# Another merge order for the retention and gated-linear mixers of a two-block network on one core

## The reference, cut to what matters

```python
def hybrid_mixer(h, hc, w_in, ret_decay, gate_up, gate_b, gla_norm_g, ...):
    lat, cx = project_in(h, w_in), project_in(hc, w_in)
    r_lat, r_ctx = bidirectional_scan(retention_inputs(lat, True), retention_inputs(cx, False))
    g_lat, g_ctx = bidirectional_scan(gla_inputs(lat), gla_inputs(cx))
    def merge(r, g, parts):
        ret = from_heads(head_layernorm(r)) * jax.nn.silu(parts[3])
        gla = from_heads(rmsnorm(g, gla_norm_g)) * jax.nn.silu(parts[7])
        return jnp.concatenate([ret, gla], axis=-1)
```

## Time and profile before

| what | us |
|---|---|
| median of three runs | 3759.76 (3759.74 to 3764.34) |
| the profiled execution, its own time | 3764.54 |
| its span in the profile | 3762.7 |
| mixer of layer 0, span time 2009.8 to 2249.9 | 240.1 |
| mixer of layer 1, span time 3127.1 to 3324.6 | 197.5 |

### The profile page before, as it was taken

How to read it: one execution, slowest core, us unless ns; L and a number is a source line. 1 busy time by engine, 2 the same in 40 slices (tenths; PEclk the granted TensorE clock), 3 DMA queues, 4 the chain that set the end, 5 groups by cost and what they waited for, 6 DMA issues and landing times.

```text
span 3762.7 us, 42305 instructions
## 1 busy us (share of the span) xinstructions
PE 3543.3 (94%) x17448; PEld 2805.7 (75%) x17448; DVE 2017.1 (54%) x3717; ACT 1232.1 (33%) x2053; POOL 212.6 (6%) x302
## 2 busy tenths in 40 slices
PE   7999899999989999998999989999998998879998
PEld 6657678887867678887986557888887885558886
DVE  5565588856654588854126664323235236654344
ACT  4353343234453333233112222332233212134332
POOL 0200000001040000000000001000001000000000
PEclk9999999999999999999999859999999998789999
DMA  4302155522202145533210011212122220112331
GB/s 164 115 12 79 45 168 179 167 91 84 74 27 78 45 157 172 168 119 124 81 57 27 26 38 46 79 57 68 57 66 86 99 68 17 40 45 90 101 91 67
DMA packets 214108, 317.01 MB, mean 84 GB/s; under 512 B 5304, under 2 KB 162618, under 8 KB 212636
## 3 DMA queue, kind: packets, MB, share of 16 engines
q1 hardware_dynamic: 198108, 243.00, 19.9%
q0 software_dynamic: 15808, 71.31, 5.6%
HBM read 300.66 MB, written 14.49 MB: 84 GB/s over the span
## 4 chain that ended last, share of the span: by engine, by line
PE 83%; DVE 11%; ACT 4%; issue 2%; DMA 1%; POOL 0%; SPq 0%; DVEq 0%; ACTq 0%; POOLq 0%
PE ps L94 82%; DVE t L115 5%; ACT t L100 3%; DVE t L107 3%; PE ps L97 1%; DVE t L111 1%; DVE ps L107 0%; DVE ps L115 0%; DVE t L121 0%; DVE t L112 0%; DMA t<-gates_away 0%; DVE t L125 0%; DVE ps L112 0%; DVE t L118 0%; DMA t<-in_mem 0%
## 5 line engine op out<-in xcount | busy, mean ns | idle before, releaser
L94 PE MATMUL ps<-t,t 128*128 128x512 f32 (+7 forms) x17032 | 3486.5, 368 | 193.5 <-DVE t L107 98.1
L94 PEld LDWEIGHTS ps<-t,t 128*128 128x128 f32 (+3 forms) x17032 | 2753.2, 191 | 900.4 <-issue 177.3
L100 ACT ACTIVATE t<-t 128x1024 fp32r<-128x1024 f32 (+6 forms) x1168 | 831.0, 744 | 1226.7 <-PE ps L94 653.5
L107 DVE TENSOR_TENSOR t<-t,t 128x1024 fp32r<-128x1024 f32 (+5 forms) x882 | 781.7, 911 | 708.9 <-ACT t L100 693.5
L100 ACT ACTIVATE t<-ps 128x512 f32<-128x512 f32 (+5 forms) x490 | 248.5, 531 | 1062.7 <-PE ps L94 1027.7
L115 DVE SCALAR_TENSOR_TENSOR t<-t,t,t 128x256 f32<-128x256 f32 (+4 forms) x935 | 438.7, 530 | 7.6 <-ACT t L100 1.2
L107 DVE TENSOR_TENSOR t<-ps,t 128x512 f32<-128x512 f32 (+4 forms) x293 | 187.4, 659 | 248.2 <-PE ps L94 181.8
L115 DVE SCALAR_TENSOR_TENSOR t<-ps,t,t 128x512 f32<-128x512 f32 (+1 forms) x228 | 139.7, 662 | 279.7 <-PE ps L94 259.6
L107 POOL TENSOR_TENSOR t<-t,t 128x64 f32<-128x64 f32 (+1 forms) x196 | 129.3, 684 | 1724.9 <-ACT t L100 1721.6
L118 DVE COPY t<-ps 128x256 f32<-128x256 f32 (+3 forms) x169 | 75.9, 477 | 276.8 <-PE ps L94 256.7
L100 ACT ACTIVATE t<-ps,t 128x512 f32<-128x512 f32 (+3 forms) x106 | 61.6, 582 | 131.9 <-PE ps L94 94.6
(11 more groups left out here) (31 smaller groups left out, 293.3 us busy)
## 6 DMA issues: line engine op xcount, KB each, us to landing
t<-in_w_ff SPq DMA_DIRECT2D x64, 1024.0 KB, 7.6
t<-in_w_mlp SPq DMA_DIRECT2D x64, 1024.0 KB, 5.4
t<-in_ada_w POOLq DMA_DIRECT2D x48, 1024.0 KB, 5.9
t<-in_w_in SPq DMA_DIRECT2D x30, 1024.0 KB, 5.3
t<-in_w_qkv_o SPq DMA_DIRECT2D x12, 1024.0 KB, 5.1
t<-in_w_mem_kv SPq DMA_DIRECT2D x8, 1024.0 KB, 6.0
t<-in_w_mem_q SPq DMA_DIRECT2D x8, 1024.0 KB, 5.1
t<-in_w_mem_o SPq DMA_DIRECT2D x8, 1024.0 KB, 5.1
```

What stands on the lines that cost most here:

```text
L94: return Issued(self, self.e and self.e.matmul(o, l, r, start=start, stop=stop, skip_group_check=True))
L100: return Issued(self, self.e and self.e.activation(o, i, f, **kw))
L107: return Issued(self, self.e and self.e.tensor_tensor(o, a, b, op))
```

## The change

`mixed_units` is replaced. Before, the retention units (61 in layer 0, 41 in layer 1) were dealt out evenly over the gated-linear units (69 and 57) less the last eight, whatever the units hold. Now only tasks count on the retention side (one each, the other retention units ride along at no cost), and gated-linear units count in parts: a work three, any other unit one. The tasks are spread evenly over all parts less eighteen, and what is left of retention comes at once when a place is reached.

```diff
     def mixed_units(l):
 
-        r, g, out_, y = ret_units(l), gla_units(l), [], 0
-        n = len(g) - 8
-        for x, u in enumerate(g):
-            out_ += [("ret", v) for v in r[y:len(r) * (x + 1) // n]] + [("gla", u)]
-            y = min(len(r), len(r) * (x + 1) // n)
+
+        parts = {"gate": 1, "cum": 1, "kv": 1, "work": 3, "sum": 1}
+        r, g, out_, y, at_g, at_r = ret_units(l), gla_units(l), [], 0, 0, 0
+        cost = [1 if u[0] == "task" else 0 for u in r]
+        whole_g, whole_r = sum(parts[u[0]] for u in g) - 18, sum(cost)
+        for u in g:
+            at_g += parts[u[0]]
+            while y < len(r) and at_r * whole_g < whole_r * at_g:
+                out_.append(("ret", r[y]))
+                at_r += cost[y]
+                y += 1
+            out_.append(("gla", u))
+        out_ += [("ret", v) for v in r[y:]]
         return out_
```

## The result

The changed kernel takes 3770.32 us (median; 3766.08 to 3782.38), the kernel before 3763.83 us on the same chip (3759.72 to 3782.35). The ratio is 1.0022, with an interval of 1.0013 to 1.0032. I had forecast 3748 with a range up to 3768: the time went the other way and ended outside the range. (The base had moved too: it was 3759.8 when I forecast, so on this one the same -12 us would read 3752.)

A forecast was written before the change was run, and what follows sets the result against it. The mixers were taken as PE-bound at a clock that falls where works stand alone, with DVE bounding states stages and layer 0's tail. Layers at -5.3 and -5.8 gave -11, kept as -12: 3759.8 - 12 = 3748 us, range 3725 to 3768.

The forecast's parts named there:

- gates: First mixer stage, both layers: shorter with less PE work, 20.5 instead of 28.3 us in layer 0, 20.6 instead of 26.7 in layer 1.
- works 0: In layer 1: 54.7 us of PE work at clock 0.85 with 5 idle, 69.4 against 63.9 us, +5.5.
- The prices of PE's work: Per-unit PE times: a work 2.7 us at 2.4 GHz and 4.7 at 1.2, a latent task 1.84, a context task 1.04.
- States 0: DVE sets this stage: 18 instead of 21.1 us in layer 0 (-3.1), no change in layer 1.
- The check on before: Prices tested on works 0 of layer 0, kernel before: 60.2 us at clock 0.82 gives 73.4, with idle 80.6 against 78.9.
- everything on PE costs double: Price claim for all PE work when the clock is 1.2 instead of 2.4 GHz, named as what is at stake.
- Works 0 of layer 0: 71.8 us of PE work after taking more tasks, at clock 0.90 with 3 us idle: 82.5 us, +3.6; bounds 74 and 95.
- rival B: The clock in works 0 stays at 0.82 and 0.79 while the stages hold more PE work: about +1, 3761 us; chance 20%.
- Works 1 of layer 0: 40.3 us of PE work at clock 0.90 with 2 idle: 46.8 instead of 40.8 us, +6; bounds 42 and 78.
- Tail: In layer 0, DVE's remaining work plus the last norm's chain: 42.8 instead of 50.8 us, -8; in layer 1, 0.
- States 1 of layer 1: Two DVE tasks less in this stage: -1.5 us.
- Rival C: Works 1 of layer 0 fall to 1.2 GHz despite tasks beside them: 78 instead of 46.8 us, 3779 in all; chance 15%.

The follow-up runs named there:

- e2: The new order in layer 1's mixer alone, the old order in layer 0: 3754.69 us, 0.9977 of the kernel before.
- e15: The new order in layer 1 alone, layer 0 as before, run again under another name: 3755.53 us, 0.9978 of the kernel before.
- e7: The changed kernel without the decay tables of heads 1 to 3 in both layers (head 0's used): 3751.15 us, 0.9962 of the kernel before.
- e9: The changed kernel with each decay table made in four pieces, one ahead of each of the head's first four tasks: 3772.82 us, 1.0029 of before.
- e14: Layer 1 in the new order; layer 0 as before but four tasks moved from the gates into works 0: 3763.62 us, 1.0001 of the kernel before.
- e12: Layer 1 in the new order, layer 0 as before, decay tables in four pieces in both layers: 3768.97 us, 1.0020 of the kernel before.
- e10: The changed kernel with the six units of layer 0's last norm dealt out between works 8 to 10 and the sums: 3770.79 us, 1.0014 of before.
- e5: The kernel before plus an unread 128x512 matmul behind each of direction 1's last six works (layer 0) and last seven (layer 1): 3762.98 us, 1.0002.
- e11: Layer 1 in the new order, layer 0 as before, plus five unread 128x512 matmuls behind works 3 to 7 of layer 1: 3762.27 us, 0.9994.
- e8: Layer 1 as changed; layer 0 with every retention unit costing 1, a work two parts, a stop of 8: 3773.66 us, 1.0025 of the kernel before.
- e13: Layer 1 new; layer 0 as before but five tasks leave states, eight instead of four beside direction 1's works, one in the tail: 3766.24 us, 1.0004.
- e16: The changed kernel run once more: 3777.85 us, 1.0036 of the kernel before.

## Why the prediction was wrong

**Layer by layer.** I had layer 0 at -5.3 us and layer 1 at -5.8; in the profiled executions they were +8.0 and -2.1. That is 17 of the 18.5 us between the forecast difference (-12) and that of the medians (+6.5). Timed in each layer alone it is sharper: +14 in layer 0, and -9 and -8 in layer 1 (e2, e15). So layer 1's forecast was about right, by errors that cancel in its stages (gates -5.3, works 0 -5.2, states 1 +13.4 against my numbers), and the failure lies in layer 0.

**The prices of PE's work and the gates: right, and better than forecast.** Gates forecast 20.5 and 20.6 us, measured 16.3 and 15.3, at a clock of 1.00 in both. States 0: 18 and 21.9, measured 18.4 and 21.7. In stages with works, though, my prices are too high: 71.8 us of PE work at the measured clock of 0.83 would be 86.5 us busy, and it was 81.3. The check on before had shown this already (73.4 against 71.7). And "everything on PE costs double" at 1.2 GHz isn't so for a work, which by my own prices goes from 2.7 to 4.7 us. (The product that I wrote as 4.4 is 4.7, so the addition for missing records had no ground; the price used is the same. 71.8 / 0.90 + 3 is 82.8, not 82.5.)

**Works 0 of layer 0: the step that failed.** I wrote 82.5 us, "PE waits for it less: I take 3 us idle and a clock of 0.90". It was 91.1. Neither assumption came: the clock was 0.83, hardly above the 0.82 of before, and the idle time 9.8 us, more than the 7.2 of before. That PE's busy time, 81.3, is near the 79.8 that I had is luck: the lower clock and the too high price cancel. I had argued from DVE's load in the stage, which hardly changed. But PE waits for single results, not for DVE's sum. Four of its six waits, of 1.1 to 1.4 us, are like those of before (four of 1.4 to 1.5); what came is 2.8 instead of 1.6 us for a copy that e7 and e9 show to stand behind head 1's table, and 1.9 us for `end` and `var` side by side. e14 moves four tasks into the stage and gets 81.3 busy and 10.3 idle.

The clock stayed where rival B had it. The Trainium skill (TensorE: Matmul & The Clock Gate, "A second HAM failure mode: psum-queue depth-cycling") says of another kernel that PE was idle for short times between groups of matmuls often enough to make the clock swing between its two levels. This trace agrees in that PE is busy for 81.33 of 91.10 us, has six short waits, and the clock is 0.83; that the waits make it swing no run here shows, and in layer 1 of e12 less idle time came with a lower clock. Rival B's length for the stage, 90.6, was right by two errors: 71.8 / 0.82 is 87.6 us of busy time, 6 more than PE had, and its 3 us idle were 7 too few. B's total of 3761 was too low all the same, since it left the other stages at my sum.

**Works 1 of layer 0.** The mechanism was right (clock 0.82 instead of 0.60), the length wrong by 5.4: 52.2 instead of 46.8, of it 6.6 idle where I took 2: the wait of 5.0 us behind head 3's table, which I hadn't seen at this place. **Tail:** 47.6 instead of 42.8. I had priced the last norm's chain at 4.5 us of DVE's standing still and added it to a tail that I took for DVE-bound; but DVE was busy for only 35.6 of 47.6. e10 shows 4.7 us of it to be the norm's place, of which works 1 took 2.6.

**States 1 of layer 1: overlooked.** I wrote -1.5 for "two DVE tasks less". It was +11.9, of it 6.1 for the block of `end` and table shown above and 4.8 for the lower clock. I had looked for such a block in works 0 (where there is one, with 8.5 us) and not here. It was paid for by gates and works 0 (64.2 us where I had 69.4).

**What the failure is as a whole.** The forecast counted the change as a matter of PE's clock, and took idle time as a small remainder. Measured in the two profiles, PE's busy time fell (-10.1 us in layer 0, -4.8 in layer 1: 158.7 to 153.9), and its idle time rose by 18.1 and 2.7. Rival C, the clock falling in works 1 of layer 0, gave the right side with the wrong mechanism: it stayed at 0.82.

**What is shown and what stays open.** Shown: layer 0 loses and layer 1 gains; in layer 0's profiles PE is busy for less time and idle, mostly behind DVE, for more; removing three tables takes 8.5 of the 18.1 us of new idle time away and 19 us from the kernel (e7); both kinds of move cost with what moves along. Not shown is that the blocks of the tables are the cause of it: cutting them up took the waits behind them away (e9, e12) and yet no time from the kernel. In layer 1 PE's busy time grew by about as much or more, at a lower clock. The other half of the idle time, `end` beside `var` on one bank and the states' chain with fewer tasks to fill it, was never taken out alone while the tasks stayed where they are. Nor was it told apart whether tasks cost more in works than in the stages that they left. And what decides when the clock falls in works 0 remains open.

## What to carry to other kernels

Write the length of a stage as busy plus idle of the engine that bounds it, and forecast both: a move that lifts the clock by spreading wide matmuls also changes what is queued ahead of single results on the other engine, and here the second was larger than the first. Don't take idle time that is removed for time that is won: in layer 1 of e12, 6 us of it went and the mixer got longer. In a merge order that gives some units a cost of zero, look at what piles up at one place. And where two parts of a program take the same change, time it in each alone: here the better kernel, 0.9977 and again 0.9978 of before, is the change in layer 1 only.

## What the runs showed of the hardware

- Extra wide matmuls behind a fall of the clock can bring it back, and need not: in layer 1 of e5 it was 0.50 from 3265.0 to 3281.8 us and 1.00 from there to the stage's end, with one filler behind each work; in works 1 of layer 0 of e5 and of layer 1 of e11 it stayed at 0.50 beside the same fillers.
- The same instructions have one of two lengths in layer 1. Its mixer in the new order took 188.9 to 189.1 us in four profiles (e2, e8, e14, e15) and 195.2 to 195.4 in four others (after, e10, e13, e16). The difference lies in works 1 where I looked: 39.8 us at a clock of 0.66 in e2, 45.7 at 0.53 in after.
- Less waiting came with a longer busy time of PE: with tables in pieces layer 1 had 35.7 and 36.3 us of idle time instead of 41.2 to 41.9, and 158.6 and 158.7 us of busy time instead of 147.0 to 154.0.
- The full clock gains less on small float32 matmuls than on wide ones: 284 against 431 ns for 64x64, and 618 against 1138 ns for 128x512.
